# Recurrence of a gated mixer: gates opened first, low part ahead of masked copies, block copies behind them

## The reference, cut to the recurrence

```python
def step(s, inp):
    kc, vc, lf = inp[0], inp[1], inp[2]
    cum = jnp.cumsum(lf, axis=2)
    last = cum[:, :, -1:, :]
    s_new = jnp.exp(last[:, :, 0, :])[..., None] * s + \
        jnp.einsum('bhsd,bhse->bhde', kc * jnp.exp(last - cum), vc)
    qc = inp[3]
    o_inter = jnp.einsum('bhtd,bhde->bhte', qc * jnp.exp(cum), s)
    diff = cum[:, :, :, None, :] - cum[:, :, None, :, :]
    decay = jnp.exp(jnp.where(mask, diff, -jnp.inf))
    att = jnp.einsum('bhtd,bhsd,bhtsd->bhts', qc, kc, decay)
    return s_new, o_inter + jnp.einsum('bhts,bhse->bhte', att, vc)

def hg_gate(z, lb):
    k = (1.0 - lb) * jax.nn.sigmoid(-z)
    log_f = jnp.log(lb + (1.0 - lb) * jax.nn.sigmoid(z))
    return k, log_f
```

## Time and profile before

| | us |
|---|---|
| median of 3 runs | 2039.65 (2030.6 to 2041.46) |
| the profiled execution | 2028.58 |
| its span | 2026.8 |
| TensorE (PE) busy | 1774.6 (88%) |
| VectorE (DVE) busy | 1297.0 (64%) |
| ScalarE (ACT) busy | 837.4 (41%) |
| GpSimd (POOL) busy | 86.3 (4%) |

### The profile page before, as it was taken

The page is one execution under the profiler, slowest core; times in us unless marked ns, Lnnn a source line. Parts: engine busy times, 40 slices in busy tenths (PEclk is TensorE's granted clock), DMA queues, the critical chain, the costliest instruction groups (busy, mean ns, idle before and its releaser), DMA issues.

```text
span 2026.8 us, 30767 instructions
## 1 busy us (share of the span) xinstructions
PE 1774.6 (88%) x12174; PEld 1591.6 (79%) x12174; DVE 1297.0 (64%) x2384; ACT 837.4 (41%) x1633; POOL 86.3 (4%) x153
## 2 busy tenths in 40 slices
PE   4799878989999999798676999967799987879997
PEld 2689767878888888697466998766799977769996
DVE  1436767558877656577575678757578884564544
ACT  2523664142322222436443444346444434554432
POOL 0000233000000000001020000000000000000000
PEclk8989888889999999898688999988899998889999
DMA  8452011045546654232334888631489873315653
GB/s 272 146 189 83 27 43 43 22 145 159 187 158 194 186 181 141 85 105 68 106 104 135 235 258 269 239 96 42 119 244 272 272 236 97 91 42 146 188 177 125
DMA packets 359118, 300.34 MB, mean 148 GB/s; under 512 B 8048, under 2 KB 333408, under 8 KB 358720
## 3 DMA queue, kind: packets, MB, share of 16 engines
q1 hardware_dynamic: 357584, 294.22, 47.4%
q0 software_dynamic: 1392, 4.15, 0.9%
HBM read 297.30 MB, written 1.05 MB: 147 GB/s over the span
## 4 chain that ended last, share of the span: by engine, by line
PE 74%; DVE 11%; DMA 5%; ACT 5%; issue 4%; SPq 0%; DVEq 0%; ACTq 0%; POOLq 0%
PE bank L902 72%; PE bank L916 3%; ACT whigh L1432 2%; DVE wlow L1877 1%; DMA raw<-in_w_up 1%; DMA AWH<-in_ada_w 1%; DMA raw<-in_ffn_w_out 1%; DVE A L1974 1%; DVE HTL L1980 1%; DVE A L2176 1%; DMA A<-in_w_ada 1%; ACT A L1607 1%; DMA X<-in_ctx 0%; DVE nmax L2145 0%; DVE A L2294 0%
## 5 line engine op out<-in xcount | busy, mean ns | idle before, releaser
L1877 DVE TENSOR_TENSOR wlow<-raw,whigh 128x2048 fp32r<-128x2048 f32 (+1 forms) x183 | 410.2, 2245 | 321.6 <-ACT whigh L1432 321.1
L1432 ACT ACTIVATE whigh<-raw 128x2048 fp32r<-128x2048 f32 (+1 forms) x183 | 343.2, 1877 | 313.6 <-PE bank L902 110.2
L902 PE MATMUL bank<-HTH,whigh 128*128 128x256 f32 (+1 forms) x1424 | 445.5, 313 | 15.5 <-DVE HTL L1980 12.5
L902 PE MATMUL bank<-HTH,wlow 128*128 128x256 f32 (+1 forms) x1424 | 441.0, 310 | 0.0
L902 PE MATMUL bank<-HTL,whigh 128*128 128x256 f32 (+1 forms) x1424 | 440.8, 310 | 0.0
L902 PE MATMUL bank<-whigh,HTH 128*128 128x256 f32 (+1 forms) x1008 | 294.6, 292 | 21.0 <-DVE HTL L1980 9.0
L902 PEld LDWEIGHTS bank<-HTH,whigh 128*128 128x128 f32 x1424 | 274.4, 193 | 29.3 <-issue 13.6
L902 PE MATMUL bank<-wlow,HTH 128*128 128x256 f32 (+1 forms) x1008 | 290.6, 288 | 0.0
L902 PE MATMUL bank<-whigh,HTL 128*128 128x256 f32 (+1 forms) x1008 | 290.4, 288 | 0.0
L902 PEld LDWEIGHTS bank<-HTH,wlow 128*128 128x128 f32 x1424 | 274.1, 192 | 13.6
L902 PEld LDWEIGHTS bank<-HTL,whigh 128*128 128x128 f32 x1424 | 274.4, 193 | 12.6
(11 more groups left out here) (208 smaller groups left out, 2231.5 us busy)
## 6 DMA issues: line engine op xcount, KB each, us to landing
raw<-in_ffn_w_in SPq DMA_DIRECT2D x88, 512.0 KB, 5.3
A<-in_ada_w SPq DMA_DIRECT2D x38, 1024.0 KB, 7.3
A<-in_w_ada SPq DMA_DIRECT2D x32, 1024.0 KB, 5.5
raw<-in_w_gate SPq DMA_DIRECT2D x44, 512.0 KB, 5.3
raw<-in_w_up SPq DMA_DIRECT2D x44, 512.0 KB, 6.3
raw<-in_ffn_w_out SPq DMA_DIRECT2D x20, 1024.0 KB, 6.2
raw<-in_w_in SPq DMA_DIRECT2D x18, 1024.0 KB, 7.2
raw<-in_w_down SPq DMA_DIRECT2D x18, 1024.0 KB, 6.8
```

The costliest lines, as they stand in the source:

```text
L902: return nc.tensor.matmul(out, lhsT, rhs, start=start, stop=stop, skip_group_check=True)
L1432: nc.scalar.activation(parts(loads[n])[0], raw_slot(loads[n]), ACT.Copy).then_inc(*made("split_high", loads[n]))
L1877: V.tensor_tensor(low, raw_slot(loads[n]), as_float(high), ALU.subtract).then_inc(*made("split_low", loads[n]))
```

## The change

ScalarE's order in step n becomes `gates_open(n+2)`, `take_decays(n+1)`, `take_tails(n+1)`, `copy_blocks(n)`, `gates_closed(n+2)`. The block copies wait for the last masked copy; the masked copies no longer wait for the block copies. VectorE's `gate_done` is parted into `own_gates` (layer 1) and `decays_low`, and in layer 0 the low part stands ahead of the masked copies, with a wait of its own for the product that last read the buffer.

```diff
@@ copy_blocks, ScalarE
                     act.wait_ge(*upto("product", "a", l, s, ROUND_END[1]))
-                    act.wait_ge(*upto("cleared", l))
-                    if n >= 2 and steps[n - 2][3]:
-                        act.wait_ge(*upto("read_out", l, s - 2))
+                    act.wait_ge(*upto("masked", l, s, MASK_ORDER[-1]))
@@ ScalarE's loop
+                    if n + 2 < len(steps):
+                        gates_open(n + 2)
                     if n + 1 < len(steps):
                         take_decays(n + 1)
-                    if n + 2 < len(steps):
-                        gates_open(n + 2)
+                    if n + 1 < len(steps):
+                        take_tails(n + 1)
                     if has_out:
                         copy_blocks(n)
-                    if n + 1 < len(steps):
-                        take_tails(n + 1)
                     if n + 2 < len(steps):
                         gates_closed(n + 2)
@@ VectorE
-                def gate_done(n):
+                def own_gates(n):
...
+                def decays_low(n):
+
+                    s, t, d, has_out = steps[n]
+                    g = s % 2
+                    if n >= 2:
+                        dve.wait_ge(*(upto("product", "sf", l, s - 2) if s - 2 < 6 else upto("product", "e", l, s - 2, 1, 1)))
                     dve.wait_ge(*upto("decays_high", l, s))
                     V.tensor_tensor(LFL[:, g, :], LF[g], as_float(LFH[:, g, :]), ALU.subtract).then_inc(*made("decays_low", l, s))
@@ mask, VectorE
-                    dve.wait_ge(*upto("blocks_copied", l, s))
@@ VectorE's loop
                     if n + 2 < len(steps):
                         gate_sum(n + 2)
+                    if n + 2 < len(steps) and l == 0:
+                        decays_low(n + 2)
                     if has_out:
                         mask(n)
                     if n + 2 < len(steps):
-                        gate_done(n + 2)
+                        own_gates(n + 2)
+                        if l:
+                            decays_low(n + 2)
```

More of the change, by code:

```diff
@@ L2321, in recurrence @@
                     gate_sum(n)
-                    gate_done(n)
+                    own_gates(n)
+                    decays_low(n)
                 for n, (s, t, d, has_out) in enumerate(steps):
```

## The result

The changed kernel takes 2063.8 us (median of 3 runs, 2057.5 to 2066.7) against 2039.65: ratio 1.0135, with an interval of 1.0096 to 1.0173. It is slower by some 24 to 28 us where 15.4 were forecast. The profiled execution took 2066.7 us, its span is 2064.9.

The account below looks back on a forecast made before the run. It took a chain of waits between engines, none of them full, to bound the two recurrences. Its terms 4.1 + 1.8 + 5.9 + 3.6 = 15.4 us on the median 2039.65 gave 2055.0 us, range 2040 to 2066.

Parts of the forecast that it names:

- Point 1: VectorE no longer waits for block copies: 11.6 us of its idle time go, worth nothing, since products end last.
- Point 2: Layer 0's low part, ahead of the masked copies, takes 0.42 us off the path behind them and is hidden.
- Point 3: Layer 0: block copies and closed gate behind the last masked copy move T back 0.82 or 0.95 us; sum 4.1.
- Rival C: Closed gate ends before masks, T 0.15 us behind the last masked copy: 3 to 10 us faster, 2033; chance 0.07.
- Point 4: Layer 0, steps 6 and 7: read waits for masks and then block copies, 1.8 us.
- Point 5: gates_open(n+2) ahead of take_decays(n+1) makes evictions late and stalls TensorE's prepare: 5.9 us, bounds 0 and about 8.
- Point 6: Layer 1: step 5 +1.5 us, steps 6 and 7 1.8, a late eviction +0.3, step 4 covered by a load; sum 3.6.
- rival B: Clock falls too behind wider TensorE gaps ahead of prepare: up to 2.4 us each, some 7 us, 2062; chance 0.15.

Follow-up runs that it names:

- e11: The changed kernel with gates_open behind take_decays again and 22 identity turns (12 where a modulation lies ahead) in TensorE's wait for the closed gate: 2046.10 us, ratio 1.0081.
- e12: The changed kernel with 22 identity turns (12 where a modulation lies ahead) in TensorE's wait for the closed gate: 2052.43 us, ratio 1.0116.
- e6: The kernel before with 8 identity turns (4 where a modulation lies ahead) in TensorE's wait for the closed gate: 2035.07 us, ratio 1.0014.
- e2: The changed kernel with gates_open(n+2) behind take_decays(n+1) again, as before the change: 2049.99 us, ratio 1.0064.
- e4: The changed kernel with layer 0's low part behind the masked copies again: 2067.11 us, ratio 1.0132.
- e1: The kernel before with only layer 0's low part moved ahead of the masked copies: 2029.22 us, ratio 0.9963.
- e3: The changed kernel with gates_closed(n+2) ahead of copy_blocks(n) on ScalarE: 2062.26 us, ratio 1.0113.
- e8: e1 plus layer 1's own gates and low part ahead of the masks, and its closed gate ahead of the block copies: 2031.29 us, ratio 0.9981.
- e7: The kernel before with only gates_open(n+2) moved ahead of take_decays(n+1): 2042.59 us, ratio 1.0039.
- e5: The changed kernel with 12 identity turns (6 where a modulation lies ahead) in TensorE's wait for the closed gate: 2055.44 us, ratio 1.0103.
- e9: e2 with 12 identity turns (6 where a modulation lies ahead) in TensorE's wait for the closed gate: 2049.71 us, ratio 1.0069.

## Why the prediction was right in direction and short in size

By the account of six cycles, the changed kernel lost 89.3 less 66.2 = 23.1 us there. It parts into three:

- serial: from products to T, e11 less before, 45.1 less 39.9 = 5.2 us;
- stalls: T to products in e12 less e11, 30.8 less 24.0 = 6.8 us, less the 1.6 that are the clock in e12's `prepare(5)`: 5.2 us;
- clock: the rest, 12.6 us: 5.8 from two sets of products at 6.24 in place of 3.34, 5.2 in `prepare` (38.4 less e12's 30.8, less the 2.4 by which e11's is shorter than before's), and that 1.6.

A second way through kernels with filled gaps gives nearly the same. e12 less e6, the changed kernel and the one before each with turns, is 75.8 less 62.1 = 13.7 us, and 1.6 of these are the clock too: 12.1 for serial part and stalls, which leaves 11.0 for the clock. So the clock's share of the 23.1 us is 11 to 13, about half.

The split is one of several kernels' differences: in the changed kernel itself the low clock hides a part of the stalls (2.3 us of idle time in three steps, where e12 has 3.8 in six), and the clock's share is what it takes beyond that. The 5.8 us of the products belong to gaps and stalls together: they are gone with the gaps filled (e12) and also with the stalls gone and the gaps open (e2). Outside these cycles layer 0 lost nothing: 1.1 us less ahead of them, the same behind.

**Point 1 (VectorE's wait is worth nothing): right.** The masked copies still start behind the products (the idle of 1.35 us at 294.49 is ended by PE, as the 0.38 of the earlier trace rows).

**Point 2 (the low part, 0.42 us, hidden): it is hidden, but worth nothing here.** e4 shows that its place makes no difference while the closed gate comes late; the 0.82 and 0.95 of point 3 don't depend on it. **Rival C was mis-priced**: I put T "0.15 us behind the last masked copy" if the closed gate came first. e1 shows T leaving the masks, 2.9 us ahead of their end; and in the changed kernel itself (e3) an early closed gate moved T under the masks and shortened nothing, since the evictions then came late. The masks were on the path only through the low part that stood behind them, on VectorE's queue. That reading was to be had from the earlier trace rows: "LFL" was the releaser.

**Point 3 (block copies and gate serial): right.** Reckoned for the steps 0 to 5: 0.82, 0.95, 0.5, 0.95, 0.82, and 0.92 for T at step 5. In e12 T lay later behind the products than before by 0.83, 0.98, 0.51, 1.03, 0.81 and 0.98 us. Of the last, all but 0.13 was to be taken up behind the readout, that is 0.8; the stretch from the T of `prepare(7)` to the products of step 6 did shrink, by 1.1 us (6.9 to 5.8).

**Point 4 (reads of steps 6 and 7, +1.8): the waits are there, the loss isn't.** TensorE waits 2.42 us for the block copies ahead of the `read` of step 6, where no wait stood before, and 3.88 in place of 2.75 ahead of that of step 7. But from the T of `prepare(7)` to its end layer 0 took 28.7 us before and after, for 2.2 us were won ahead of these reads: the 1.1 of point 3, and 1.1 in the products of step 6 (4.46 us from 345.07 on the earlier trace rows, now 3.34). The second was not foreseen and is luck with the clock.

**Point 5 (stalls behind `gates_open`, 5.9): right in mechanism, near in size.** e12 less e11, step by step: 1.1, 0.9, 0.6, 1.1, 2.3, 0.9, against 1.2, 1.0, 0, 1.5, 0.7, 1.5. The 2.3 holds 1.6 of low clock and 0.7 of stall, so the stalls sum to 5.2. The reckoned 0 for step 2 rested on a low clock that hides the stall: in the changed kernel no row of that step shows one, and at full clock (e12) it is 0.6.

**Point 6 (layer 1, +3.6): half shown.** Step 5, the worst: masks end at 1065.41, T at 1068.43, so 3.0 us in place of 1.38, +1.6 where +1.5 was reckoned.

```profile
1065.51 0.94 ACT L1729 ACTIVATE A<-bank 64x256 f32<-64x256 f32 x3 [6.67 <-DVE A L2298]
...
1067.74 0.42 DVE L2257 TENSOR_TENSOR LFL<-A,LFH 128x256 fp32r<-128x256 f32 x1
...
1068.43 0.66 PE L916 MATMUL bank<-ident,A 128*128 128x128 f32 x2 [3.52 <-ACT modc L1474]
```

The 7.6 us of the profile are more, but one set of products at 6.24 us in step 7 is 2.9 of them, and e1, whose layer 1 is that of before but for a wait that is long met, shows 101.9 us against 95.0. How much of layer 1's loss is the change's stays open to some 5 us either way.

**The step that failed is the one left out: the clock, rival B.** "The sum above leaves it out" was the error: the sum put it at nothing, and in layer 0 it measured 11 to 13 us, the largest term of the three. The rows for it were in hand: gaps of 1.63 and 1.41 us ahead of fast `prepare`, of 2.60 ahead of a slow one, and a reckoned delay of 0.8 to 0.95 for each. In e2 the 1.63 became 2.98 and `prepare(2)` went from 3.77 to 5.29 us; the 1.10 ahead of `prepare(6)` (at 328.12 before) became 1.95, and it went from 3.51 to 5.13. Filled to 1.05 and 0.55 (e11) they took 3.80 and 3.78. Not every gap that B named fell by itself: ahead of `prepare(4)` the 1.41 became 1.95 and it stayed fast in e2; in the changed kernel its clock fell only behind its stall (at 314.12). B's price of 2.4 us a fall was right for `prepare` as an upper end (1.5 to 1.6 here), but it had no term for the products: 2.9 us for each set, twice, and both behind a stall inside `prepare` (at 314.12 and 348.12). By the rule that the prediction cited from the Trainium skill, page "TensorE: Matmul & The Clock Gate", section "Why this matters for your kernels", that idle gaps put the array back to the low clock, the trace agrees again, in kind. With B in the sum, 4.1 + 1.8 + 5.9 + 3.6 + 7 = 22.4, the forecast would have been 2062. That this is near the measured 2063.8 is in part luck: B's 7 us were too few for layer 0, and the 1.8 of point 4 was won back.

## What to carry to other kernels

When a copy moves behind another engine's last work, look at what stands behind it on the same in-order engine (here the closed gate, and in e3 the evictions), and ask of each such thing who waits for it. When every cycle of a loop gets a wider gap on TensorE, put the clock's price into the sum, for the matmuls behind the gap and for those behind a stall within them; it was larger here than the delay itself. And when a gap between two engines closes, look for the next place where the same engine comes early (the readout in e8): the gain was only seen in the time once that was moved as well.

## What the runs showed of the hardware

- The same 56 products (64x64) took 3.34 us in most steps, 6.24 in some, and 3.6 to 6.0 in a few. In the changed kernel the steps 1, 2, 4 and 6 had gaps of 2.5 to 3.6 us ahead of `prepare` and no stall in it: `prepare` was slow, its products took 3.34. Step 0 had a stall of 0.82 and no gap: 3.34. Steps 3 and 5 had a gap of 1.95 and a stall of 0.82 and 0.66: 6.24. In e12, with filled gaps, stalls of up to 0.82 were followed by 3.34 throughout steps 0 to 5. That looks as if it took both; but in e7 the products of step 2 took 6.24 behind a gap of 2.61 us and a `prepare` without a stall. What slows the products is open.
- The length of the gap alone does not say whether `prepare` runs slow. Ahead of `prepare(4)` e5 and e9 both had six turns and then 1.21 to 1.22 us of idle time: in e5 its matmuls of 512 columns took 0.39 to 0.50 us, in e9 0.61 to 0.71. Gaps of 1.41 and 1.63 us were followed by fast ones before, and one of 2.25 in e9 too.
- A low part on VectorE (128x256) takes 0.42 us alone and 0.77 to 0.95 where GpSimd works on the same kind of tile beside it, here in e2:

```profile
291.10 0.66 POOL L830 TENSOR_TENSOR A<-A,own_sum 128x256 f32<-128x256 f32 x1 [1.97 <-DVE A L2321]
291.20 0.83 DVE L2257 TENSOR_TENSOR LFL<-A,LFH 128x256 fp32r<-128x256 f32 x1
```

- A stretch whose code is the same, layer 1's recurrence, took 95.0 us in the profile of before and 101.9 in that of e1 (stretch, busy times and clock as in the earlier trace rows):

```profile
962.80:1065.10 102.30, 71.50 (x576) 56.61 (x576) 60.76 (x169) 43.40 (x123) 17.77 (x38) 0.70 0.32 104
```

TensorE was busy 71.5 us at 0.70 against 65.9 at 0.77. A single profile of such a stretch settles no difference of 5 us; layer 0's six cycles, where e4 repeats the changed kernel's to 0.1 us, are on firmer ground, but before's were profiled once.
